# Two seven-product pairs of feed-forward steps in each stage instead of one

## The reference, cut to what matters

```python
def swiglu(x, w_in, w_out):
    gate, up = jnp.split(x @ w_in, 2, axis=-1)
    return (jax.nn.silu(gate) * up) @ w_out
# x: 256 x 1024, w_in: 1024 x 5632 (gate and up of 2816 each), w_out: 2816 x 1024, all float32
x = x + 0.5 * swiglu(rms_norm(x, ffn1_norm_g[i]), ffn1_w_in[i], ffn1_w_out[i])   # and ffn2; twice
# the third layer has one more of the same size: w_gate, w_up, w_down
```

## Time and profile before

| | |
|---|---|
| median of 3 runs | 1532.05 us (1531.9 to 1535.41) |
| the profiled execution's own time | 1531.57 us |
| its span, first to last instruction | 1529.8 us |
| PE busy | 1517.7 us, 99% |
| DVE busy | 1094.3 us, 72% |
| ACT busy | 858.6 us, 56% |
| POOL busy | 358.5 us, 23% |
| granted TensorE clock | 0.999 |
| loaded from HBM | 295.92 MB, 194 GB/s over the span |

### The profile page before, as it was taken

One profiled execution on the slowest core, in us unless ns is written; L12 is line 12 of the kernel. 1 busy time (PEld: TensorE's weight loads), 2 busy tenths in 40 slices (PEclk: granted clock), 3 DMA queues, 4 the chain that ended last, 5 costly groups with the idle time before them and its releaser, 6 DMA issues.

```text
span 1529.8 us, 19935 instructions
## 1 busy us (share of the span) xinstructions
PE 1517.7 (99%) x7906; PEld 1292.2 (84%) x7906; DVE 1094.3 (72%) x1174; ACT 858.6 (56%) x1075; POOL 358.5 (23%) x256
## 2 busy tenths in 40 slices
PE   9999999999999999999999999999999999999998
PEld 7888888888778888888888888899988899888886
DVE  6677766557778567776776678599998566666875
ACT  7545554645365454556776456476887343464554
POOL 0352200001732135320001631100571000017320
PEclk9999999999999999999999999999999999999999
DMA  7977665457776688765416986766554665578763
GB/s 253 314 243 233 188 182 188 138 170 211 239 246 192 193 275 251 228 195 173 158 56 206 285 230 203 209 191 204 181 181 147 212 192 187 173 223 273 226 194 102
DMA packets 274309, 311.43 MB, mean 204 GB/s; under 512 B 64272, under 2 KB 233512, under 8 KB 274216
## 3 DMA queue, kind: packets, MB, share of 16 engines
q1 hardware_dynamic: 273112, 308.84, 64.4%
q10 hardware_dynamic: 1104, 1.31, 0.3%
HBM read 295.92 MB, written 1.09 MB: 194 GB/s over the span
## 4 chain that ended last, share of the span: by engine, by line
PE 90%; POOL 3%; DVE 2%; issue 2%; DMA 2%; ACT 2%; ACTq 0%; DVEq 0%; POOLq 0%
PE ps L2344 22%; PE ps L2348 22%; PE ps L2345 22%; PE ps L2334 3%; PE ps L2336 3%; PE ps L2335 3%; PE ps L2546 2%; PE ps L2545 2%; PE ps L2544 2%; DMA scr<-scr 1%; PE ps L2387 1%; PE ps L2500 1%; POOL scr L750 1%; DVE w_lo L1412 1%; POOL scr L760 0%
## 5 line engine op out<-in xcount | busy, mean ns | idle before, releaser
L1412 DVE TENSOR_TENSOR w_lo<-w_raw,w_hi 128x2048 fp32r<-128x2048 f32 x250 | 598.5, 2400 | 185.1 <-ACT w_hi L803 184.7
L803 ACT ACTIVATE w_hi<-w_raw 128x2048 fp32r<-128x2048 f32 x250 | 477.0, 1912 | 250.8 <-PE ps L2348 200.5
L2344 PE MATMUL ps<-w_hi,xg_hi 128*128 128x512 f32 (+1 forms) x960 | 375.2, 391 | 1.2 <-DVE scr L1527 1.2
L2348 PE MATMUL ps<-w_hi,xg_lo 128*128 128x512 f32 (+1 forms) x960 | 372.1, 388 | 0.0
L2345 PE MATMUL ps<-w_lo,xg_hi 128*128 128x512 f32 (+1 forms) x960 | 372.0, 387 | 0.0
L750 POOL COPY scr<-scr 128x512 uint16<-128x512 uint16 x100 | 121.1, 1231 | 697.8 <-DVE scr L1527 697.7
L2344 PE MATMUL ps<-w_hi,y_hi 128*128 128x512 f32 x666 | 261.9, 393 | 1.3 <-DVE y_lo L1532 0.7
L2348 PE MATMUL ps<-w_hi,y_lo 128*128 128x512 f32 x666 | 259.1, 389 | 0.0
L2345 PE MATMUL ps<-w_lo,y_hi 128*128 128x512 f32 x666 | 258.9, 389 | 0.0
L2344 PEld LDWEIGHTS ps<-w_hi,xg_hi 128*128 128x128 f32 x960 | 180.3, 188 | 39.1 <-DVE w_lo L1412 1.6
L2348 PEld LDWEIGHTS ps<-w_hi,xg_lo 128*128 128x128 f32 x960 | 180.3, 188 | 36.8
(11 more groups left out here) (403 smaller groups left out, 1710.8 us busy)
## 6 DMA issues: line engine op xcount, KB each, us to landing
w_raw<-in_ffn_w_in_dram SPq DMA_DIRECT2D x168, 512.0 KB, 5.0
w_raw<-in_ffn_w_out_dram SPq DMA_DIRECT2D x88, 512.0 KB, 5.5
w_raw<-in_w_in_dram SPq DMA_DIRECT2D x82, 512.0 KB, 4.6
w_raw<-in_a_w_in_dram SPq DMA_DIRECT2D x28, 512.0 KB, 4.5
w_raw<-in_w_down_dram SPq DMA_DIRECT2D x22, 512.0 KB, 5.1
w_raw<-in_w_gate_dram SPq DMA_DIRECT2D x21, 512.0 KB, 4.1
w_raw<-in_w_up_dram SPq DMA_DIRECT2D x21, 512.0 KB, 5.2
y_raw<-in_ffn_w_in_dram SPq DMA_DIRECT2D x16, 512.0 KB, 5.4
```

The costliest lines, as they stand in the source:

```text
L803: act.activation(w_hi[:, u % RING, :], w_raw[:, u % RING, :], ACT.Copy).then_inc(w_rounded, 1)
L1412: dve.tensor_tensor(w_lo[:, s, :], w_raw[:, s, :], w_hi[:, s, :].bitcast(F32), ALU.subtract).then_inc(w_split, 1)
L2344: pe.matmul(dst, xh, hi, start=start, stop=False, skip_group_check=True)
L2348: return pe.matmul(dst, xl, hi, start=False, stop=stop, skip_group_check=True)
```

## The change

The pairs start at steps 4 and 8 of every stage instead of at step 7. The sums of x are made by DVE instead of POOL, in step 1. The weight-sum buffers are used once for each pair, the sums of x serve both. A stage has 31 units instead of 32. On DVE the sums T1, T3 and T2 of a pair p stand together, in step p-2 (for the second pair at the end of the first pair), ahead of the split of G(p-1,1); T4 and the low part of T1 stand in step p-1, and the low part of T2 now at the head of the pair.

```diff
-PAIR = 7
+PAIRS_OF = ((4, 8),) * 5
+def ffn_places(pairs):
+    order, i = [("G", 0, 0), ("G", 0, 1)], 1
+    while i < NI:
+        if i in pairs:
+            order += [("G", i, 0), ("G", i, 1), ("G", i + 1, 1), ("D", i - 1), ("G", i + 2, 0), ("G", i + 2, 1), ("D", i), ("D", i + 1)]
+            i += 3
+        else:
+            order += [("G", i, 0), ("G", i, 1), ("D", i - 1)]
+            i += 1
+    return {step: k for k, step in enumerate(order + [("D", NI - 1)])}
...
 # SP, a step; p is the first pair's step (4)
+                    gate_up(1, i)
+                    if i == p - 2:
+                        block(p, 1, 1)
+                    down(i - 1)
+                    if i == p - 3:
+                        block(p, 0, 0)
+                    if i == p - 1:
+                        block(p, 3, 0)
+                    if i < NI - 1:
+                        gate_up(0, i + 1)
+                    turn_back(i - 1)
+                    if i == p - 3:
+                        block(p, 0, 1)
+                        block(p, 1, 0)
+                    if i == p - 2:
+                        block(p, 2, 0)
+                        block(p, 2, 1)
+                    if i == p - 1:
+                        block(p, 3, 1)
+                    if i + 1 in pairs[1:]:
+                        block(i + 1, 3, 0)
+                        block(i + 1, 3, 1)
 # SP, in the pair; q is the second pair's step (8)
                     turn_back(p)
+                    if q:
+                        block(q, 0, 0)
+                        block(q, 0, 1)
...
                     turn_back(p + 1)
+                    if q:
+                        for k in (1, 2):
+                            block(q, k, 0)
+                            block(q, k, 1)
...
 # POOL
-                    if i == 1:
-                        x_sums()
-                    if i == 2:
-                        s_sums()
...
 # ACT, a step
                     round_(v + 2)
                     hidden_high(i - 1, (i - 1) % 2)
-                    if i == 4:
-                        t_high(T1, f"T1 {f}")
-                    if i == 5:
+                    if i + 1 in pairs:
+                        t_high(i + 1, T1, "T1")
+                    if i + 1 == pairs[0]:
                         s_high()
                     round_(v + 3)
                     for tt in range(2):
                         silu(i, tt)
-                    if i == 5:
-                        t_high(T2, f"T2 {f}")
+                    if i + 1 in pairs:
+                        t_high(i + 1, T2, "T2")
                     round_(v + 4)
...
 # DVE, a step
                     split(v + 2)
                     hidden_low(i - 1, (i - 1) % 2)
                     if more:
                         next(extra, None)
-                    if i == 3:
-                        t_sum(T1, T3, T1, "T1")
-                    if i == 4:
-                        t_sum(T3, T2, T3, "T3")
-                    if i == 5:
-                        t_sum(T4, T4, T2, "T4")
-                    if i == 6:
-                        t_low(T2)
+                    if i == pairs[0] - 3:
+                        x_sums()
+                    if i + 1 in pairs:
+                        t_sum(i + 1, T4, T4, T2, "T4", "T2")
                     split(v + 3)
                     for tt in range(2):
                         product(i, tt)
                     if more:
                         next(extra, None)
...
+                    if i == pairs[0] - 3:
+                        s_sums()
+                    if i + 2 in pairs:
+                        t_sums(i + 2)
+                    if i + 1 in pairs:
+                        t_low(i + 1, T1)
+                    if i + 1 == pairs[0]:
+                        s_lows((0, 1))
                     split(v + 4)
                     if more:
                         next(extra, None)
+                def x_sums():
+
+                    dve.tensor_tensor(x_sum, xg_hi[:, :, :].bitcast(F32), xg_lo[:, :, :].bitcast(F32), ALU.add).then_inc(vec_done, vec(f"X {f}"))
+
+                def s_sums():
+
...
+                    dve.wait_ge(vec_done, vec.at(f"X {f}"))
+                    dve.tensor_tensor(s1, a21, a22, ALU.add).then_inc(vec_done, vec(f"S1 {f}"))
+                    dve.tensor_tensor(s3, a11, a21, ALU.subtract).then_inc(vec_done, vec(f"S3 {f}"))
+                    dve.wait_ge(vec_done, vec.at(f"S1 {f}"))
+                    dve.tensor_tensor(s2, s1, a11, ALU.subtract).then_inc(vec_done, vec(f"S2 {f}"))
+                    dve.wait_ge(vec_done, vec.at(f"S2 {f}"))
+                    dve.tensor_tensor(s4, a12, s2, ALU.subtract).then_inc(vec_done, vec(f"S4 {f}"))
+                def t_sums(p):
+                    t_sum(p, T1, T3, T1, "T1")
+                    t_sum(p, T3, T2, T3, "T3", "T1")
+                    t_sum(p, T2, T2, T1, "T2", "T3")
 # DVE, the pair
+                    t_low(p, T2)
                     split(n + 2)
+                    if p == pairs[0]:
+                        s_lows((2, 3))
+                    t_low(p, T3)
+                    t_low(p, T4)
...
                     split(n + 8)
+                    if p + 4 in pairs:
+                        t_sums(p + 4)
+                    if p + 2 == NI - 1:
+                        hidden_low(p + 2, p % 2, tiles(ps[:, 6, :]))
                     split(n + 9)
```

More of the change, by code:

```diff
@@ L106, in plan_units @@
     add("w_o", "dddd")
-    add("ffn4", ffn)
+    add("ffn4", ffn[4])
     return first, opens
@@ L310, in bank @@
         def bank(u):
-            return 4 + (u + sum(u > U[f"ffn{f}"] + 3 * NI - 2 for f in range(5))) % RING
+            return 4 + (u + sum((3 * NI - len(PLACES[f])) * (u >= U[f"ffn{f}"] + len(PLACES[f])) for f in range(5))) % RING
         def turn_bank(n, k):
@@ L346, in build, with alone_until, alone @@
         T1, T3, T2, T4 = range(4)
+        def alone_until(f, i):
+            def alone(f, j):
+                return j not in PAIRS_OF[f] and j - 1 not in PAIRS_OF[f]
+            return sum(alone(g, j) for g in range(f) for j in range(NI)) + sum(alone(f, j) for j in range(i + 1))
         x_sum = tiles(KB(40, 8))
@@ L534, in ffn @@
                     small_inputs()
-                for i in range(1, PAIR):
-                    gate_up(1, i)
-                    down(i - 1)
-                    if i == 1:
[L539 to L564, removed]
+                i = 1
+                while i < NI:
+                    if i in pairs:
+                        pair(i)
+                        i += 3
+                    else:
+                        step(i)
+                        i += 1
+                if NI - 3 not in pairs:
+                    down(NI - 1)
                 if f == 4:
@@ L974, in ffn @@
                         act.activation(rope[:, j], rope[:, j], ACT.Sin).then_inc(act_done, act_(f"rope {j}"))
-                for i in range(3, PAIR):
-                    step(i)
-                pair()
-                for i in range(PAIR + 3, NI):
-                    step(i, last=i == NI - 1)
+                i = 3
+                while i < NI:
+                    if i in pairs:
+                        pair(i)
+                        i += 3
+                    else:
+                        step(i)
+                        i += 1
             def mem(n, gain):
@@ L2594, in ffn, with step @@
+                def step(i):
                     gates(i, taken(i - 1))
@@ L2596, in ffn @@
                         pe.wait_ge(act_done, act_.at("M kT 1"))
-                    down(i - 1, start=i == 1)
-                pair()
-                for i in range(PAIR + 3, NI):
-                    gates(i, taken(i - 1))
-                    down(i - 1, hidden=(lambda: hidden(NI - 1)) if i == NI - 1 else None)
+                    down(i - 1, start=i == 1, hidden=(lambda: hidden(NI - 1)) if i == NI - 1 else None)
+                i = 1
+                while i < NI:
+                    if i in pairs:
+                        pair(i)
+                        i += 3
+                    else:
+                        step(i)
+                        i += 1
                 down(NI - 1, norm=n + 1)
```

275 lines of the change are left out of this document (134 added, 141 removed).

## The result

The changed kernel takes 1556.63 us, the median of 4 runs (1553.89 to 1559.45), against 1533.29 us for the kernel before (4 runs, 1531.9 to 1535.41). The ratio is 1.0151, with a 95% interval of 1.0127 to 1.0175. It is slower, as forecast, but by 23 us and not by 8, and it lies outside the range of 1522 to 1550.

A forecast was written before the change was run, and what follows sets the result against it. The prediction took PE's own pace as the bound, with DVE's added work making PE late. Stages 0 to 4 summed as 0.9+3.7+1.7+1.7+0.4 = +8.4 us on 1531.57, forecast 1540, with an 8-in-10 range of 1522 to 1550.

The forecast's parts named there:

- one more pair gives 13.6 us: On PE's path: 12 matmuls less in each of five stages, 5 x 2.72 = 13.6 us saved.
- stage 1's 3.0: PE in stage 1: 3.0 us lost before the change, which may go because their place is re-ordered.
- steps 1 and 2: DVE in stage 3: sums of x cost nothing; join(1) 1.5 us later from the ring; G(3,1) 2.2 us late.
- the plan: PE's gapless schedule for stage 3, 5.44 us a unit: 38.1 us from D(0) to M1, expected 40.3 after the change.
- Steps 3 and 4: DVE from G(3,1)'s split to the low part of T2, stage 3: M6 4.4 us late in all, 2.2 of it new.
- without a break: DVE from G(3,1) to M6 in stage 3: it owes 16.5 us where PE needs 16.3, so it must work continuously.
- the clock left to the upper end: PE's waits: a longer wait could drop TensorE's clock; counted in the range's upper end alone, no size given.
- the second pair: Pair at step 8: covered by 1.9 us at G(7,1) and 1.6 at the low part of T2, nothing lost.
- The third rival: Second pair late as well: T1 waits 4 us in the ring, each stage loses 2.1 us more, 1550; chance 0.15.
- All hidden: Rival: all work added to DVE fits in its idle time, 1531.6 - 16.6 = 1515 us; chance 0.10.
- The order costs, the ring doesn't: Rival: block(1,0) lands in idle DMA time, join(1) and join(2) don't move, -6.8 us: 1525; chance 0.17.
- my 24.9: Predicted lateness of M6 in first pairs, stages 0 to 4: 3.6, 9.4, 4.4, 4.4, 3.1, sum 24.9 us.

The follow-up runs named there:

- experiment 11: The changed kernel with POOL's cuts and joins of steps 1 to 9 copying 8 of 128 columns, output not the reference's: 1531.8 us, one run.
- experiment 1: The changed kernel with the first pair's three weight sums on DVE behind the split of G(3,1) instead of ahead of it: 1556.98 us.
- experiment 6: The changed kernel with PE doing the second unit's block ahead of M6 instead of behind it, in both pairs: 1546.81 us, one run.
- experiment 7: The changed kernel with the high and low parts of S1 to S4 moved to the head of step 2: 1544.76 us, one run.
- experiment 2: The changed kernel with added matmuls, results unused, where PE waited ahead of G(3,1) and M6, to keep the clock up: 1554.41 us.
- experiment 5: The changed kernel with block(1,1) of the first pair issued behind turn_back(1) instead of ahead of it: 1556.46 us, one run.

## Why the prediction was right and wrong

1. **Right: one more pair gives 13.6 us, and stage 1's 3.0 go.** The span closes within 0.7 us with both.
2. **Right: steps 1 and 2.** The sums of x cost nothing. Join(1) was to come 13.0 us behind D(0) in stage 3 and came 12.87. The wait ahead of G(3,1) was put at 2.2 us there and was 2.78. Of the 0.6 more, 0.35 is idle time ahead of T3, 0.48 us where it is 0.13 in the other stages. It isn't the cut: in experiment 11 the same 0.48 stands there with the cut over 0.41 us before; its cause stays open. In stages 0 and 2 join(2) comes a little earlier against DVE and falls on the very split of G(3,1) (590.73 beside 591.55), which makes 3.8. From D(0) to M1 PE took 42.6 us in stage 3 and not 40.3: 2.8 of wait and 1.7 of pace lost behind it, which the plan didn't have.
3. **Wrong: the size of the step "Steps 3 and 4", the chain from that split to the low part of T2.** This is the step that failed. Its arithmetic was 4.4 us in stage 3 and the measured lateness of M6 is 6.75. Of the missing 2.4, 2.2 are two meetings with a join. I had named the rule and priced it where rows of before showed it, for cuts beside sums; the joins I let run in 1.34 us and cost DVE nothing. Join(2) was released at 28.2 us behind D(0), where I had put it (28.7), but it ended 1.0 us late. By the stage's rows ACT's rounding and DVE's next split are then 1.06 late, and the low part of T2 beside join(3) adds 1.1; the rest is the 0.15 from its end to M6's start. That low part was held in all five first pairs. Experiment 11 shows that without these meetings the rows shrink and M6 starts earlier, and the kernel with the pair at 8 alone has M6 waiting 1.0 us just in the three stages whose low part met a join. A chain that I myself had called "without a break" has no place where a copy could be served free of cost.
4. **Wrong: the clock left to the upper end.** In the changed kernel waits of 2.24 us (2.08 in the profile's rows) and more at G(3,1) or M6 were each followed by 3.41 us at the lower level, seven places and eight stretches (two in a row in stage 1, from 2.2 us before its wait of 4.4 us ended); waits of 1.55 us (1.39) and less were not. That is no rule: by the rows of experiments 1, 6 and 7, waits of 3.16, 3.05 and 2.69 us left the clock at 1.00, and in experiment 2 it fell behind one of 1.78. M6's own wait in stage 3 is charged to ACT at 902.98 and to DVE elsewhere, but it ends each time with DVE's low part of T2. For the time this mattered nearly only behind M6, 5.1 us by the table (38.6 - 33.5): ahead of it the lost pace shortens the wait at M6 (in stages 0 and 2 it uses it up and adds 0.2 us), as experiment 2 shows, where keeping the clock gave back 3 of 13.6 us.
5. **Wrong by 3.0: the second pair.** I had it covered by 1.6 us at the low part of T2; each second pair lost 0.5 to 0.7. No join held that part (2.28 us in all five stages). In stage 3 join(6) took 1.69 us instead of 1.34, and the low part of T1 and the split behind it took 0.6 more beside a cut; the rest of some 2.1 us isn't traced. With the small copies of experiment 11 the second pairs lost nothing. The third rival's loss, 2.1 us in each second pair, did not happen.
6. **The rivals.** "All hidden" was far off. "The order costs, the ring doesn't" is refuted by join(1), and experiment 5 shows that even without that delay the time is the same. (Its sum has a slip: with -1.8 and -2.5 a stage it is -6.4 and not -6.8, which rounds to the same 1525.) Against the forecast of 1540.0 the profiled execution has 15.9 us more: 8.6 at M6 over my 24.9, 5.1 for the clock behind it and 3.0 in the second pairs, less 0.8 spread elsewhere.

What stays open: how much of stage 1's 11.7 us is the angles and how much its late join(1); the move of the sines ran only together with others.

## What to carry to other kernels

When one engine's chain is the late one, price every meeting with an engine that it shares something with, not only those that the trace of before happens to show: the change moves instructions into new neighbourhoods. In this chain undoing one wait (order, ring or clock: experiments 1, 2 and 5) moved the wait and not the time; taking work out of the chain or moving the consumer behind it (6, 7, 11) moved the time, by 10 to 25 us. The work crowded near the start of a stage cost more than the same work later in it (33.1 against 9.3 us for one pair a stage).

## What the runs showed of the hardware that was not expected

A POOL copy of 0.21 us took 2.21 beside a sum of two SBUF inputs, and a join of 1.34 us took 3.44 where a split had begun 0.06 us before it (stage 2 of the changed kernel):

```profile
634.28 2.29 DVE L1442 TENSOR_TENSOR w_lo<-w_raw,w_hi 128x2048 fp32r<-128x2048 f32 x1 [0.87 <-ACT w_hi L827]
634.34 3.44 POOL L799 COPY scr<-scr 128x1024 uint16<-128x1024 uint16 x1 [3.71 <-DMA scr<-scr]
```

The one that starts later pays what is left of the other, whatever its own size.

In the changed kernel the half clock came in stretches of 3.41 us (one of 6.83), each at a wait of PE (the program's last microseconds aside), and much of its loss was paid back by a shorter wait later. But not every long wait brings it. Here is one that didn't, ahead of G(3,1) in stage 2 of experiment 6, and the clock behind it (1.00):

```profile
594.16 0.50 PE L2402 MATMUL ps<-w_hi,xg_hi 128*128 128x512 f32 x1 [3.05 <-DVE w_lo L1442]
594.10:600.00 5.90, 5.84 (x26) 4.83 (x27) 5.90 (x5) 4.69 (x8) 0.00 (x0) 1.00 0.80 247
```

A mean granted clock of 0.990 against 0.999 looked like 14 us, and was worth 3 where the clock alone was restored.
